# Sample keys turned by VectorE in 32x32 blocks, with four cache pages side by side in the four partition blocks

## The reference, cut to what matters

```python
phys_page = page_table[bidx, pidx // PAGE_SIZE]
k_sel = where(is_past, cache_k[l, phys_page, offset], k_new[bidx, nidx])
v_sel = where(is_past, cache_v[l, phys_page, offset], v_new[bidx, nidx])
s = einsum('bthd,btkhd->bthk', q, k_sel) * HEAD_DIM ** -0.5     # masked outside the picked keys
a = einsum('bthk,btkhd->bthd', softmax(s), v_sel)
```

## Time and profile before

| | us |
|---|---|
| median of three runs | 1219.84 (1217.93 to 1219.89) |
| the profiled execution, its own time | 1214.59 |
| its span in the trace | 1212.5 |
| PE busy in the span | 1179.9 (97%) |
| DVE, ACT, POOL busy | 597.2, 359.0, 354.1 |
| the sample stage, from the first turned keys to the last values | 632.7 to 991.7 |

### The profile page before, as it was taken

The page is one execution under the profiler, slowest core; times in us unless marked ns, Lnnn a source line. Parts: engine busy times, 40 slices in busy tenths (PEclk is TensorE's granted clock), DMA queues, the critical chain, the costliest instruction groups (busy, mean ns, idle before and its releaser), DMA issues.

```text
span 1212.5 us, 26754 instructions
## 1 busy us (share of the span) xinstructions
PE 1179.9 (97%) x10300; PEld 1087.3 (90%) x10300; DVE 597.2 (49%) x1083; ACT 359.0 (30%) x665; POOL 354.1 (29%) x150
## 2 busy tenths in 40 slices
PE   6999999999999999999989999999999999999995
PEld 6888889999999999999987889888889879999992
DVE  3666658874665657451444622623523552323226
ACT  4333333223323323322333322322323342122210
POOL 2432222333333334334311311311321223333310
PEclk9999999999999999999999999999999999999996
DMA  7543143233232223354226857857867656222203
GB/s 250 130 121 80 48 111 89 70 88 89 79 104 82 80 79 98 93 154 129 62 85 196 287 208 245 300 194 250 287 207 248 214 189 219 82 76 86 69 1 147
DMA packets 197975, 170.50 MB, mean 141 GB/s; under 512 B 19890, under 2 KB 178538, under 8 KB 196658
## 3 DMA queue, kind: packets, MB, share of 16 engines
q1 hardware_dynamic: 184458, 160.48, 42.7%
q10 hardware_dynamic: 13424, 8.67, 2.4%
HBM read 159.47 MB, written 9.74 MB: 140 GB/s over the span
## 4 chain that ended last, share of the span: by engine, by line
PE 91%; DVE 6%; issue 1%; DMA 1%; ACT 1%; DVEq 0%; SPq 0%; ACTq 0%
PE acc L1138 67%; PE bank L1438 5%; PE bank L1454 3%; PE acc L1525 3%; PE bank L1196 2%; PE bank L1332 2%; PE bank L1313 2%; DVE scoreP L1793 1%; PE acc L1579 1%; DVE top L1789 1%; PE acc L1483 1%; DMA xnat<-in_x_prompt 1%; PE bank L1248 1%; DVE y L2185 1%; PE bank L1322 1%
## 5 line engine op out<-in xcount | busy, mean ns | idle before, releaser
L634 POOL TENSOR_TENSOR wL<-rawW,wH 128x1024 fp32r<-128x1024 f32 (+1 forms) x146 | 353.9, 2425 | 811.4 <-ACT wH L656 811.4
L1138 PE MATMUL acc<-actH,wH 128*128 128x272 f32 (+1 forms) x2304 | 491.5, 294 | 1.2 <-DVE actL L1707 1.2
L1138 PE MATMUL acc<-actH,wL 128*128 128x272 f32 (+1 forms) x2304 | 476.6, 288 | 0.0
L1138 PE MATMUL acc<-actL,wH 128*128 128x272 f32 (+1 forms) x2304 | 475.0, 288 | 0.0
L1138 PEld LDWEIGHTS acc<-actH,wH 128*128 128x128 f32 (+1 forms) x2304 | 360.1, 188 | 23.9 <-issue 21.9
L1138 PEld LDWEIGHTS acc<-actL,wH 128*128 128x128 f32 (+1 forms) x2304 | 361.4, 188 | 0.0
L1138 PEld LDWEIGHTS acc<-actH,wL 128*128 128x128 f32 (+1 forms) x2304 | 359.1, 188 | 0.0
L656 ACT ACTIVATE wH<-rawW 128x1024 fp32r<-128x1024 f32 (+1 forms) x146 | 153.7, 1054 | 226.2 <-PE acc L1138 210.3
L2120 DVE SCALAR_TENSOR_TENSOR y<-y,bank 128x512 f32 (+1 forms) x16 | 11.0, 688 | 122.3 <-PE bank L1647 120.4
L1438 PE MATMUL bank<-sq,kPage 128*128 128x128 f32 x480 | 65.6, 280 | 4.1 <-DVE kPT L1951 4.0
L1438 PEld LDWEIGHTS bank<-sq,kPage 128*128 128x128 f32 x480 | 52.9, 142 | 14.5 <-issue 9.8
(11 more groups left out here) (207 smaller groups left out, 1019.6 us busy)
## 6 DMA issues: line engine op xcount, KB each, us to landing
rawW<-in_w_in SPq DMA_DIRECT2D x112, 512.0 KB, 3.8
vPage<-in_cache_v SPq DMA_DIRECT2D x64, 512.0 KB, 4.8
kPage<-in_cache_k SPq DMA_DIRECT2D x60, 512.0 KB, 4.6
rawW<-in_w_out SPq DMA_DIRECT2D x32, 512.0 KB, 4.1
y<-in_x_prompt SPq DMA_DIRECT2D x4, 1024.0 KB, 9.3
out_y_prompt<-y SPq DMA_DIRECT2D x8, 512.0 KB, 2.8
xnat<-in_x_prompt SPq DMA_DIRECT2D x2, 1024.0 KB, 7.9
xnat<-in_x_prompt ACTq DMA_DIRECT2D x2, 1024.0 KB, 10.9
```

Source lines behind the costliest of these rows:

```text
L634: pool.tensor_tensor(wL[:, slot, :, 0:width], rawW[:, slot, :, 0:width], wH[:, slot, :, 0:width].bitcast(F32), ALU.subtract).then_inc(stag ...
L1138: last = pe.matmul(acc[t.slot][0:width, e, 0:HT], w[:, u.slot, k, 0:width], a[:, kk, e * HT:(e + 1) * HT], start=(half == 0 and k == 0 and ...
```

## The change

The keys are no longer turned by PE. A "unit" of keys is now 64 positions (two streaks of 32) of four pages, and the four pages (`SIDES`) lie in the four blocks of 32 partitions. Each unit is brought by four DMAs, each of 64 rows of 4 KB into 32 partitions. DVE transposes the unit in place, in blocks of 32x32 (2 instructions of 128x1024). After that a partition block holds a quarter of a head's 128 dimensions for its own page, and the 32 columns of a block are keys. The queries are laid out to match: `qBlock` holds, for every head and every quarter of the dimensions, 32 columns in which the four pages have 8 columns each (`queries`, 8 small copies per sample; `qAll` is a copy of the queries with every quarter of the dimensions in every partition block, made once by 16 DMAs from SBUF to SBUF). A unit's products are 32 matmuls with 64 keys moving. The scores of a sample stand as 128x288: 4 pages x 2 x 4 rows in each block of 32 partitions are all used. The softmax must join the four partition groups, which `over_sides` does for the maximum and for the sum, with small DVE operations. `probs_turned` has 3 transposes.

On SP a unit of keys now waits for the products of the unit in its place (`k_done`), and each of its four page numbers is loaded after that wait, right before its DMA. `dropD`, from which the mask is read, is written by 11 DMAs of SP, where one of ACT did it.

The core of the diff:

```diff
+SIDES = 4
+STREAK = P // SIDES
+UNITS = 4
+HP = PAST // SIDES
+LP = HP + NS
@@ SP
-            def key_pages(x, pair, behind, g=None):
-                i, at = (None, 0) if g is None else (g, g)
-                t = turn(4 * x + pair, 2, i, 8)
-                pages = [page_number(ck, (2 * at + x) * PAGES + (2 * pair + e)) for e in range(2)]
-                if behind is not None:
-                    b = bb(behind, g)
-                    sp.wait_ge(bank_full[b.slot], b.full)
-                for e in range(2):
-                    load_page(ck, kPage[:, 1 - t.slot, e, :, :].rearrange("p h d -> p (h d)"), pages[e], k_in[t.slot])
+            def key_unit(x, n, done, g=None):
+                i, at = (0, 0) if g is None else (g, g)
+                sp.wait_ge(k_done, 2 * UNITS * i + done)
+                for side in range(SIDES):
+                    page = page_number(ck, (2 * at + x) * PAGES + (SIDES * (n // 2) + side))
+                    rows_of = ck[ds(page, 1), 2 * STREAK * (n % 2):2 * STREAK * (n % 2 + 1), :]
+                    sp.dma_start(kPage[STREAK * side:STREAK * (side + 1), 1 - n % 2, :, :, :].rearrange("p e h d -> p e (h d)"),
+                                 rows_of.rearrange("a (e p) n -> p (a e) n", e=2)).then_inc(k_in[n % 2], 16)
...
+            sp.wait_ge(qs_ready, 1)
+            for side in range(SIDES):
+                for j in range(SIDES):
+                    sp.dma_start(qAll[STREAK * side:STREAK * (side + 1), j, :],
+                                 qS[STREAK * j:STREAK * (j + 1), :, :].rearrange("p h n -> p (h n)")).then_inc(q_spread, 16)
             sp.wait_ge(exp_ready, 32)
-            first_key_page(3, 0)
-            first_key_page(3, 1)
-            value_page(0, 1)
-            value_page(0, 2)
+            first_key_part(3, 0)
+            first_key_part(3, 1)
+            sp.wait_ge(drop_ready, 1)
+            for side in range(SIDES):
+                for a in range(HALF):
+                    sp.dma_start(dropD[side, a, :, 0:HP].rearrange("r (h n) -> r h n", h=2),
+                                 scoreS[:, 0:PAST].rearrange("r (h s n) -> r h s n", h=2, s=SIDES)[:, :, side, :]
+                                 ).then_inc(drop_out, 16)
...
+            mask(0, None)
+            unit(4)
             sp.wait_ge(c_done, 1)
             sp.dma_start(wtab[:], windows).then_inc(wtab_in, 16)
-            mask(0, None)
-            unit(4)
-            key_pages(1, 0, "K3a")
-            value_page(0, 3)
+            value_page(0, 0)
+            key_unit(1, 0, 1)
+            value_page(0, 1)
             unit(5)
             pool_loads(0)
-            key_pages(1, 1, "K15a")
+            value_page(0, 2)
+            value_page(0, 3)
+            key_unit(1, 1, UNITS)
@@ ACT
-            act.wait_ge(drop_ready, 1)
-            act.dma_start(dropD, scoreS[:]).then_inc(drop_out, 16)
...
-                key_copied("b", 1, g)
-                key_copied("b", 2, g)
@@ PE
+            def key_products(X, n, g=None):
+                i, x, b = 0 if g is None else g, "abc".index(X), bb(f"S{X}", g)
+                pe.wait_ge(k_turned, 2 * UNITS * i + UNITS * x + n + 1)
...
+                for e, keys in enumerate(key_parts(n, X == "a")):
+                    w = keys.shape[1] * STREAK
+                    at = 2 * STREAK * n + e * w
+                    for a in range(HALF):
+                        for d in range(SIDES):
+                            for j in range(QUARTERS):
+                                row = (QUARTERS * a + j) * P + d * STREAK
+                                q = (QUARTERS * a + j) * SIDES * STREAK + d * STREAK
+                                last = pe.matmul(bank[b.slot][j * SPAN:(j + 1) * SPAN, at:at + w], qBlock[:, q:q + SPAN],
+                                                 keys[:, :, row:row + STREAK], start=(a == 0 and d == 0),
+                                                 stop=(a == HALF - 1 and d == SIDES - 1))
+                last.then_inc(k_done, 1)
...
                 for m in range(PAGES):
-                    if m + 1 < 8:
-                        keys_turned("b", m + 1, g)
                     if m in (0, 2, 3, 4, 5):
                         quarter((7, 0, 8, 9, 10, 11)[m], g)
...
-                    key_products("b", m, g)
+                    if m % 2 == 0:
+                        key_products("b", m // 2, g)
+                    if m == 6:
+                        new_keys("b", g)
                     value_page("a", m)
-                new_keys("b", g)
@@ DVE
+            def keys_turned(X, n, g=None):
...
+                    dve.wait_ge(k_in[n % 2], 16 * SIDES * (4 * i + 2 * (x - 1) + n // 2 + 1))
+                    parts = [kPage[:, 1 - n % 2, e, :, :].rearrange("p h d -> p (h d)") for e in range(2)]
+                dve.transpose(parts[0], parts[0])
+                dve.transpose(parts[1], parts[1]).then_inc(k_turned, 1)
+            def over_sides(dst, src, op):
+                own.step(dve.transpose(rows[:, 3, :], src))
+                own.wait()
+                own.step(dve.tensor_reduce(fewest[:], rows[:, 3, :].rearrange("p (s r) -> p r s", s=SIDES), AX.X, op))
+                own.wait()
+                own.step(dve.tensor_copy(rows[:, 3, :].rearrange("p (s r) -> p s r", s=SIDES),
+                                         fewest[:].unsqueeze(1).to_broadcast([P, SIDES, HALF * NT])))
+                own.wait()
+                return dve.transpose(dst, rows[:, 3, :])
...
+                if late:
+                    own.step(dve.memset(outside[0:NS, 0:NS], MASKED))
+                    own.wait()
+                    dve.tensor_scalar(scoreS[:], scoreS[:], PICKED / 1.5, MASKED, ALU.is_gt, ALU.mult).then_inc(drop_ready, 1)
+                    own.step(dve.memset(qPad[:], 0.0))
+                    own.step(dve.memset(rows[:], 0.0))
+                    own.wait()
+                    keys_turned("a", 0)
+                    queries(0)
+                    keys_turned("a", 1)
+                    keys_turned("a", 2)
                 if i:
                     gated(1, range(TT))
```

More of the change, by code:

```diff
@@ new lines, in key_parts @@
+            def key_parts(n, first):
+                if not first:
+                    return [kPage[:, 1 - n % 2, :, :, :].rearrange("p e h d -> p e (h d)")]
+                if n == 2:
+                    return [first_keys(n, e).unsqueeze(1) for e in range(2)]
+                if n == 1:
+                    at = H * T
+                    return [mixed[:].rearrange("p k t -> p (k t)")[:, at:at + 2 * H * P].rearrange("p (e n) -> p e n", e=2)]
+                return [kPage[:, 1 - n // 3, :, :, :].rearrange("p e h d -> p e (h d)")]
@@ L990, in _ @@
             copy_tile(0)
-            for m in range(8):
-                key_copied("a", m)
             exps(0)
@@ L1421, in quarter @@
                 unit(TILE_B + n // 4, n // 2 % 2, g, 4, quarters=(n % 2,))
-            def keys_turned(X, m, g=None):
-                k = turn(4 * "abc".index(X) + m // 2, 2, g, 8)
-                if m % 2 == 0:
-                    if X == "a":
-                        pe.wait_ge(first_k_in[m // 2], 32)
-                    else:
-                        pe.wait_ge(k_in[k.slot], 32 * (k.full - 2))
-                for n in (2 * m, 2 * m + 1):
-                    b = bb(f"K{n}{X}", g)
-                    dst = take(b)
-                    for e in range(2):
-                        h = 2 * (n % 4) + e
-                        for a in range(2):
-                            page = first_keys(m // 2, a) if X == "a" else kPage[:, 1 - k.slot, a, :, :].rearrange("p h d -> p (h d)")
-                            last = pe.transpose(dst[:, (2 * e + a) * P:(2 * e + a + 1) * P], page[:, h * P:(h + 1) * P], ident)
-                    full(b, last)
@@ L1608, in group @@
                 for m in range(PAGES):
-                    if not last and m + 1 < 8:
-                        keys_turned("c", m + 1, g)
                     if m == 0:
@@ L1616, in group @@
                         pool_mix((m - 1) // 2, "ps"[(m - 1) % 2])
-                    if not last:
-                        key_products("c", m, g)
+                    if not last and m % 2 == 0:
+                        key_products("c", m // 2, g)
+                    if not last and m == 6:
+                        new_keys("c", g)
                     if last and m == 5:
@@ new lines, in softmax_end @@
+            def softmax_end(X, g=None, ahead=True):
+                i, x = 0 if g is None else g, "abc".index(X)
+                dve.wait_ge(mask_in[x % 2], 16 * QUARTERS * (i + x // 2 + 1))
+                b = bb(f"S{X}", g)
+                src = bank_wait(dve, b)
+                stand_alone(dve)
+                dve.tensor_tensor_reduce(probS[:], src[:, 0:LP], probS[:], -SCALE, 3e38, ALU.add, ALU.min,
+                                         rows[:, 0, 0:1]).then_inc(bank_free[b.slot], 1)
+                dve.wait_ge(bank_free[b.slot], b.read)
```

(16 more changed lines are left out.)

333 lines of the change are left out of this document (131 added, 202 removed).

## The result

The changed kernel takes 1252.66 us (median of four runs, 1243.31 to 1257.6); before takes 1218.88 (1217.87 to 1219.89) in the same comparison. The ratio is 1.0268, with a 95% interval of 1.0199 to 1.0337: 34 us slower, where 7 us less had been forecast, and outside the forecast range. The profiled execution took 1256.65 us. An execution over 1.5% above its kernel's fastest is left out of the ratios; this concerns one, in the last of the experiments.

A forecast was written before the change was run, and what follows sets the result against it. PE bounds the sample stage before, loads after, at 86.5 us per group. 10 us saved between first and last `probs_turned`, plus 0.7 behind, minus 3 at the start, say 7 off 1219.8: 1213 us, range 1177 to 1238.

The forecast's parts named there:

- PE's products: Sample stage: a unit's 32 matmuls take PE 1.04 us, four units 4.2 us.
- DVE's transposes: Sample stage: 8 of 128x1024 per sample at 1.4 us each, 11 us per sample; DVE has room, costed at nothing.
- Behind the last `probs_turned`: After the last such row, 0.7 us are saved in the last sample's transposes.
- The loads' term: Sample stage: key loads into 32 partitions take 5.5 us per unit instead of 2.5, upper bound 5.8; group 86.5 us.
- The signs named beforehand: Sample stage: DMA share near 1.0 at 240 to 260 GB/s if loads bind; under 0.9 for the slow rival.
- the slow rival: Sample stage: SP's single order leaves the DMA queue empty; group 93 us, total 1235 us; chance 0.30.
- The upper end of the range: Whole kernel: at most 1238 us; a unit at 5.8 us meant a group of 88.9 us, no gain.
- The clock as "inside the next wait": PE's clock may fall after waits for keys; the 1.6 us of work lost vanish in the next wait while loads bind.
- The start: Start of the sample stage: SP's path delays `hist`, landed near 657; `probs_turned` at about 662, 3 us lost.
- The fast one: Sample stage: 32-partition loads not slower, or SP's 5 us per unit the floor; group 73 to 76, total 1173 us; chance 0.20.
- The saving on PE: Sample stage: PE gets 16.8 us back per group, which by PE alone would last 72 us.

The follow-up runs named there:

- the last of the experiments: Four runs on the changed kernel with finer DMAs or page numbers kept; its last, four DMAs per unit in order 0, 1, 2, 3, took 1238.29 us.
- the run with page numbers ahead: Changed kernel with a unit's four page numbers loaded ahead of its wait on k_done; 1253.38 us, ratio 1.029.

## Why the prediction was wrong

The resource was the right one: loads into 32 partitions decide, and PE waits. Its price was not, and the sign hung on that.

- **PE's products: right.** A unit takes 1.03 to 1.07 us by the chain (forecast 1.04):

```profile
732.30 1.03 PE bank L1432 x64
733.33 0.44 PE acc L1492 x16
```

- **DVE's transposes: right in effect.** 1.2 us each instead of 1.4, and DVE stays below half busy in the stage (44.26 of 99.3 us). `gated(1)` began at 635.50 (forecast 636):

```profile
634.38 1.20 DVE L1861 STREAM_TRANSPOSE raw<-raw 128x1024 f32<-128x1024 f32 x1
635.50 0.45 DVE L1917 SCALAR_TENSOR_TENSOR mixed<-bank,gate 128x128 f32<-128x128 f32 x2
```

- **Behind the last `probs_turned`: right**, 1.0 us for 0.7.
- **The loads' term: the step that failed.** "For that I take 5.5 us" a unit, from 180 GB/s with a discount for four blocks, upper bound 5.8. With the share's time, a group of the changed kernel has 0.90 x 99.3 = 89 us; less the 64 - 8 x 2.5 = 44 of all else, that is 5.7 us per unit. Over all three groups (656 to 960, share 0.95) it is 6.3. With the queue full, as in the run with page numbers ahead, it is 99 x 1.00 - 44 = 55, 6.9 us per unit, or 1.05 MB / 6.9 = 152 GB/s, below the row of 180. One row of one DMA, behind which stood other work, was taken for a bound on a mix. Between 5.5 and 6.9 lie 11 us per group, nearly the whole gap from 86.5 to 99. These are estimates, for the share counts an engine as busy also when it moves little; read by the share alone, the changed kernel's group would be 1 to 2 us of dearer units and some 10 of idle queue. Single microseconds at full share read 178 and 202 GB/s as well as 339; the low ones fit the key DMAs that SP issued from 786 to 790 and from 794 to 800, if the queue is served in order, and 339 the values and weights between them:

```profile
791.00:792.00 1.00, 1.00 (x15) 0.93 (x8) 1.00 (x1) 0.00 (x0) 0.94 (x1) 1.00 1.10 178
...
799.00:800.00 1.00, 0.00 (x0) 0.00 (x0) 1.00 (x2) 0.00 (x0) 0.00 (x0) 0.51 1.19 339
...
804.00:805.00 1.00, 1.00 (x27) 0.43 (x20) 0.90 (x5) 0.00 (x0) 0.00 (x0) 0.50 1.01 202
```

  178 GB/s are 5.9 us a unit, about the upper bound of 5.8, and what more the 6.9 hold is open: the queue in order, with one half of the partitions busy at a time, is supported by the two orders of the same DMAs in the changed kernel (22 us) and hardly by those with page numbers kept (4 us), and no run measured a unit by itself.
- **The signs named beforehand: neither fits.** The load term was to show a share near 1.0 and 240 to 260 GB/s, the slow rival a share under 0.9. The group above has 0.90 at 217 GB/s, the three groups 0.95 at 225. Only the runs with other loads tell the two apart. PE waits 17.5 us per group for the 14 forecast, but only in part for keys: from 600 to 1030 us 27.2 for keys, 27.5 for `hist` and 16.2 for ACT.
- **The upper end of the range: too near.** Group 88.9 ("no gain at all") was the worst that the load term allowed, because the bound for the unit was the same row as its value. A bound needs another source. 7 us per unit would have put 99 us per group, and 1255, inside.
- **The clock as "inside the next wait": neither refuted nor shown.** PE stood idle from 794.9 to 800.8; the granted clock reads 0.51 in the last whole microsecond of that and 0.50 (1.2 GHz) at 804 (the last two windows above). No run separates what this costs.
- **The start: wrong in size, with little consequence.** I had forecast 3 us lost, 11.6 were. The wrong step is SP's: 16 DMAs from SBUF to SBUF at 0.34 us each, 5.4 in all. They took 10.15, which shifts what is behind by 4.7; `hist` was issued at 659 instead of 653 and landed at 665 instead of 657.

```profile
618.20 10.15 SPq L567 DMA_DIRECT2D mixed<-qS  x16
629.21 8.80 SPq L492 DMA_DIRECT2D kPage<-in_cache_k  x8
638.05 4.35 SPq L575 DMA_DIRECT2D dropD<-scoreS  x8
...
659.05 1.22 SPq L531 DMA_DIRECT2D hist<-in_state_pool  x2
```

- **The rivals.** The fast one is out: `kPage` does not land like `vPage` did, and PE is at 82%. The slow one gave the right sign (group 93, 1235). As it was told, an empty queue behind SP's waits, the page numbers' run speaks against it: the queue was filled and nothing changed. Not all of it is out: SP's single order is a floor at 79 us per group when the loads are cheap, and with half of the page numbers gone the same narrow loads in the same order took 1231 to 1244 us in three of four executions.
- **The saving on PE** was near: 88.9 - 74.5 = 14.4 us per group by the run with almost no key bytes, for 16.8. It is worth nothing in a group that the loads hold.

## What to carry to other kernels

When a change makes the runner-up dearer, the price of that resource decides the sign, and one undisturbed row for it is a value, not a bound: ask what the neighbours in its queue do and leave the range open on the dear side. The layout with 32 partitions per load cost here 46 us, where the rest of the change gave 11 to 12; if it must be, try loads that follow each other into different halves of the partitions, and fewer page numbers. And before believing that a removed bottleneck leaves only the next one, write down the floor of every engine for one period, the issuing one too: here PE had 72 to 75, SP 79 and the loads 89 to 99 us.

## What was not expected of the hardware

- 64 partitions were as slow as 32 for a key DMA (1253.1 and 1252.7 us), 128 (with 2 KB rows) were 46 us faster over 28 units, 1.6 us a unit.
- The order of equal DMAs in one queue was worth 22 us, and 4 us where page numbers were kept.
- The issue of a DMA held SP up to 4.75 us in the changed kernel, 0.33 in the median.
- The DMAs from SBUF to SBUF occupied SP 0.63 us each (16 in 10.15), twice the 0.34 of a load of the earlier trace rows.
- The DMA share is no measure of room: 0.90 and 1.00 went with the same group time, and the changed kernel's four executions lie 1.1% apart, where those of before lie 0.2% apart.
